# Eight conditioning units a layer ahead of the up phase, and 17 more value units by seven products

## What is computed

```python
# first block, layers i = 0, 1
x = x + mixed @ w_out[i]                       # mixer's output projection
h = rms_norm(x, norm2_w[i])
g, u = jnp.split(h @ w_up[i], [D_FF], axis=-1) # 1024 -> 2 * 2816
g = depthwise_conv_centered(g, ffn_conv_w[i], ffn_conv_b[i])
x = x + (jax.nn.silu(g) * u) @ w_down[i]       # 2816 -> 1024

# second block, layers i = 0..3; the conditioning c is the same for all tokens
shift1, scale1, gate1, shift2, scale2, gate2 = adaln(c, ada_w[i], ada_b[i])  # silu(c) @ w + b, 1024 -> 6 * 1024
h = x * (1.0 + scale1) + shift1
y = mixer_i(h)
x = layer_norm(DN_ALPHA * x + (1.0 + gate1) * y, ...)
h = x * (1.0 + scale2) + shift2
y = conv_ffn(h, ...)                           # gates and values both convolved
x = layer_norm(DN_ALPHA * x + (1.0 + gate2) * y, ...)
```

## Time and profile before

| | us |
|---|---|
| median of 3 runs | 2404.84 |
| lowest and highest | 2402.72, 2406.2 |
| profiled execution, its own time | 2405.74 |
| profiled execution, span in the trace | 2403.9 |
| TensorE busy in the span | 2379.8 |
| VectorE busy | 1636.7 |
| ScalarE busy | 729.3 |
| GpSimd busy | 151.8 |

### The profile page before, as it was taken

The page is one execution under the profiler, slowest core; times in us unless marked ns, Lnnn a source line. Parts: engine busy times, 40 slices in busy tenths (PEclk is TensorE's granted clock), DMA queues, the critical chain, the costliest instruction groups (busy, mean ns, idle before and its releaser), DMA issues.

```text
span 2403.9 us, 42597 instructions
## 1 busy us (share of the span) xinstructions
PE 2379.8 (99%) x17844; PEld 2186.9 (91%) x17844; DVE 1636.7 (68%) x3084; ACT 729.3 (30%) x1473; POOL 151.8 (6%) x268
## 2 busy tenths in 40 slices
PE   9999999999999999999999999999999999999998
PEld 7878999987899998999998899998899999889998
DVE  6653887566289947698744499954477984638983
ACT  3441220144321121533132243223423431544321
POOL 2000010000022000010000021021000000000000
PEclk9999999999999999999999999999999999999999
DMA  7935887574398756498654398754334555335542
GB/s 218 243 88 175 302 293 251 147 188 119 106 310 286 271 180 187 159 314 297 201 174 135 107 324 286 254 186 121 116 114 157 174 168 167 107 110 171 163 163 97
DMA packets 403273, 458.43 MB, mean 191 GB/s; under 512 B 50751, under 2 KB 374776, under 8 KB 403084
## 3 DMA queue, kind: packets, MB, share of 16 engines
q1 hardware_dynamic: 370098, 340.53, 45.4%
q0 software_dynamic: 29936, 112.73, 13.0%
q10 hardware_dynamic: 3050, 2.46, 0.4%
HBM read 451.48 MB, written 1.29 MB: 188 GB/s over the span
## 4 chain that ended last, share of the span: by engine, by line
PE 95%; DVE 2%; issue 1%; DMA 1%; ACT 0%; ACTq 0%; DVEq 0%; SPq 0%
PE job_bank L1034 34%; PE job_bank L1110 33%; PE job_bank L1089 11%; PE mix_bank L1089 4%; PE job_bank L1616 4%; PE mix_bank L1535 1%; PE job_bank L1118 1%; PE mix_bank L1563 1%; PE job_bank L1591 1%; PE mix_bank L1577 1%; PE mix_bank L1065 1%; PE mix_bank L1907 0%; PE job_bank L1340 0%; PE mix_bank L2011 0%; DMA sb_ring<-in_ffn_w_down 0%
## 5 line engine op out<-in xcount | busy, mean ns | idle before, releaser
L1034 PE MATMUL job_bank<-sb_h,sb_ring 128*128 128x256 f32 (+1 forms) x2880 | 645.8, 381 | 0.3 <-DVE sb_h L3375 0.3
L1034 PEld LDWEIGHTS job_bank<-sb_h,sb_ring 128*128 128x128 f32 (+1 forms) x2880 | 535.8, 189 | 83.3 <-issue 11.4
L3066 DVE SCALAR_TENSOR_TENSOR sb_arena<-sb_arena,sb_c_act 128x1024 f32<-128x1024 f32 x168 | 215.3, 1282 | 4.2
L3180 DVE SCALAR_TENSOR_TENSOR sb_arena<-sb_arena,sb_par 128x256 f32<-128x256 f32 x440 | 204.4, 505 | 8.8 <-ACT sb_arena L2189 4.9
L1110 PE MATMUL job_bank<-sb_t,sb_ring 128*128 128x128 f32 x1536 | 203.6, 275 | 1.2 <-DVE sb_ring L3116 1.2
L1110 PE MATMUL job_bank<-sb_h,sb_ring 128*128 128x128 f32 x1440 | 190.5, 275 | 0.0
L1110 PEld LDWEIGHTS job_bank<-sb_t,sb_ring 128*128 128x128 f32 x1536 | 187.3, 192 | 1.4 <-DVE sb_ring L3116 1.4
L1089 PE MATMUL job_bank<-sb_h,sb_ring 128*128 128x128 f32 x1600 | 184.1, 275 | 1.4 <-ACT sb_h L2502 1.4
L1110 PEld LDWEIGHTS job_bank<-sb_h,sb_ring 128*128 128x128 f32 x1440 | 179.2, 192 | 4.3 <-issue 1.6
L1089 PEld LDWEIGHTS job_bank<-sb_h,sb_ring 128*128 128x128 f32 x1600 | 181.2, 192 | 1.8 <-issue 1.6
L1110 PE MATMUL job_bank<-sb_t,sb_arena 128*128 128x128 f32 x1320 | 174.9, 275 | 0.8 <-DVE sb_arena L3121 0.8
(11 more groups left out here) (530 smaller groups left out, 3346.9 us busy)
## 6 DMA issues: line engine op xcount, KB each, us to landing
sb_arena<-in_ada_w POOLq DMA_DIRECT2D x96, 1024.0 KB, 7.1
sb_ring<-in_ffn_w_up SPq DMA_DIRECT2D x88, 1024.0 KB, 5.2
sb_ring<-in_w_up SPq DMA_DIRECT2D x44, 1024.0 KB, 7.1
sb_ring<-in_ffn_w_down SPq DMA_DIRECT2D x32, 1024.0 KB, 5.4
sb_ring<-in_w_in SPq DMA_DIRECT2D x24, 1024.0 KB, 6.6
sb_ring<-in_w_down SPq DMA_DIRECT2D x16, 1024.0 KB, 5.6
sb_ring<-in_hg_w_in SPq DMA_DIRECT2D x16, 1024.0 KB, 5.5
sb_ring<-in_ml_w_up SPq DMA_DIRECT2D x16, 1024.0 KB, 5.6
```

What stands on the lines that cost most here:

```text
L1034: mm = pe.matmul(o, st, mv, start=(k0 + k == 0 and t == 0), stop=(k0 + k == kn - 1), skip_group_check=True)
L3066: ins = vec.scalar_tensor_tensor(out=o, in0=w, scalar=col, in1=o, op0=ALU.mult, op1=ALU.add)
L3180: ins = vec.scalar_tensor_tensor(out=o, in0=fraw[:, i % 2, v, j:j + T], scalar=pcol(column, (l * FFN_TAPS + j) * width + c), in1=o, op0=AL ...
```

## The change

**Eight units early.** Of each layer's 24 conditioning units 8 (7 in the third layer, `ADA_EARLY`) are done before the up phase: for the first and second layer beside the mixer's output projection (5, 2 and 1 units ahead of the three additions to `x`); for the third layer 2 in the down phase of the second layer, 2 at the start of the conformer's mixer, 2 and 1 ahead of the additions of its output projection; for the fourth layer 2 in the down phase of the third, 2 and 2 in the HGRN2 mixer, 2 in its output projection. 12 (13 in the third) remain beside the up phase and 4 (`ADA_LATE`) beside the down phase. The early units of the first two layers have three buffers of their own, in a region that the scan has done with.

**The sums on TensorE** are placed by a rule now: the sums whose units are early come right after the first pair, the others four places behind the place at which VectorE is due to have counted the fourth, but no later than after the last unit (`min(p + 4, FT - 1)`). The sum of units 17 to 20 moves from the down phase to that last place.

**GpSimd** issues the loads of the early units when the first unit of the output projection is used, and `tap_loads` and `gate_loads` only after them. The products that follow stand directly behind these loads now, each ahead of the load of unit 8, 9 and so on.

**17 more fast value units.** 4 in each layer of the first block (values 1 to 9 are all fast), 5 in the second block's layer 0 (1, 3, 5, 7, 9) and 4 in its layer 1 (2, 4, 6, 8). In the second block VectorE joins such a value's tiles, where ScalarE copied them out of the bank before.

```diff
-ADA_BESIDE_UP = 20
+ADA_EARLY = (8, 8, 7, 8)
+ADA_LATE = 4
 FAST_FROM = 2
-FAST_VALUES = (1, 3, 5, 7, 9)
+FAST_VALUES = {1: ((1, 2, 3, 4, 5, 6, 7, 8, 9),) * L1, 2: ((1, 3, 5, 7, 9), (2, 4, 6, 8))}
...
+        def ada_place(layer, c):
+            if layer < L1 and c < ADA_EARLY[layer]:
+                return ADA_RING + c % ADA_RING
+            if c < ADA_EARLY[layer] or c >= ADA_UNITS - ADA_LATE:
+                return 1 + (c + 1) % 2
+            return c % ADA_RING
...
+        def ada_beside(layer, p):
+            beside = ADA_UNITS - ADA_EARLY[layer] - ADA_LATE
+            return p * beside // FT
+        def ada_ready(layer, count):
+            if count <= ADA_EARLY[layer]:
+                return -1
+            return next((p for p in range(FT) if ADA_EARLY[layer] + ada_beside(layer, p + 1) >= count), None)
...
                 if layer < L1:
                     ssd_rows(layer)
-                pool.wait_ge(s.tail_x, 2 * layer + 1)
-                if layer == L2 - 1:
-                    gate_loads()
-                if layer == L1 - 1:
-                    tap_loads()
+                    pool.wait_ge(s.unit_used, plan[("out1", layer)][0][1][0][0] + 1)
                 beside = tap_weights() if layer == L1 - 1 else gate_weights() if layer == L2 - 1 else iter(())
                 for c in range(ADA_UNITS):
+                    if layer == L2 - 1 and c == 6:
+                        pool.wait_ge(s.ho_read, 4)
+                    if c == ADA_EARLY[layer]:
+                        pool.wait_ge(s.tail_x, 2 * layer + 1)
+                        if layer == L2 - 1:
+                            gate_loads()
+                        if layer == L1 - 1:
+                            tap_loads()
                     if c >= 8:
                         next(beside, None)
...
+                layer = l if stack == 1 else l + 2
+                ready = [ada_ready(layer, 4 * (r + 1)) for r in range(ADA_UNITS // 4)]
                 def condition(n):
-                    if n in (8, 12, 17, 21):
-                        ada_quad()
+                    if n == 1:
+                        pe.wait_ge(s.tail_x, 2 * layer + 1)
+                    for p in ready:
+                        if p is not None and n == (1 if p < 0 else min(p + 4, FT - 1)):
+                            ada_quad()
...
                 first_products(d2, 2, *over_f(2))
-                ada_quad()
+                if ready.count(None) > 1:
+                    ada_quad()
...
                 for i, job in enumerate(plan[("out1", l)][:-1]):
+                    ada_units((5, 2, 1)[i])
                     add_to_x(job, i)
...
-            branch_out("pw2", 2, 0)
+            branch_out("pw2", 2, 0, (2, 1))
```

More of the change, by code:

```diff
@@ L466, in build @@
         zs = ssd(KD, T)
+        scanned_at = ssd.at
         yssm = ssd(KD, T)
@@ L505, in build @@
         ffn(8 * UC)
+        ffn(ARENA - ffn.at - (ADA_RING * 2 + 2) * ADA_COLS_AT_ONCE - UC)
         ada_w = ffn(ADA_RING, 2, ADA_COLS_AT_ONCE)
@@ L508, in build @@
         ada_rows = ffn(UC)
-        ada_buffer = [c % 3 if c < ADA_BESIDE_UP else 1 + (c + 1) % 2 for c in range(ADA_UNITS)] * L2
+        first_at = scanned_at - ADA_RING * 2 * ADA_COLS_AT_ONCE
+        ada_first = arena[:, first_at:scanned_at].rearrange("p (b k c) -> p b k c", b=ADA_RING, k=2)
+        def ada_place(layer, c):
[4 more added lines that the diff above has]
+            return c % ADA_RING
+        ada_buffer = [ada_place(layer, c) for layer in range(L2) for c in range(ADA_UNITS)]
+        ada_tile = [ada_w[:, b, :, :] if b < ADA_RING else ada_first[:, b - ADA_RING, :, :] for b in ada_buffer]
         ada_before = [max((m for m in range(n) if ada_buffer[m] == b), default=None) for n, b in enumerate(ada_buffer)]
-        ada_landed = [16 * ada_buffer[:n + 1].count(b) for n, b in enumerate(ada_buffer)]
+        ada_signal = [b % ADA_RING for b in ada_buffer]
+        ada_landed = [16 * ada_signal[:n + 1].count(b) for n, b in enumerate(ada_signal)]
         half_k = 4
@@ L655, in fast_up @@
             gates, values, _ = glu_jobs(stack, l)
-            if stack == 2 and l < FAST_FROM:
-                return gates[1:]
-            return [job for i in range(1, FT // 2)
-                    for job in (gates[i], values[i]) if job is gates[i] or stack == 2 or i in FAST_VALUES]
+            return [job for i in range(1, FT // 2) for job in (gates[i], values[i])
+                    if job is gates[i] or stack == 2 and l >= FAST_FROM or i in FAST_VALUES[stack][l]]
         def fast_down(stack, l):
@@ L1287, in fast_ups @@
                 heads(ups[:2], norm, before, ns)
+                after(1)
                 over_h = (h[:, :, :], hform, tform_no(stack, l))
@@ L3050, in ada_unit @@
                 n = ada_n[0]
-                vec.wait_ge(ada_in[ada_buffer[n]], ada_landed[n])
+                vec.wait_ge(ada_in[ada_signal[n]], ada_landed[n])
                 if n % 4 == 0 and n >= 8:
@@ L3056, in ada_unit @@
                 for k in range(2):
-                    w = ada_w[:, ada_buffer[n], k, :]
+                    w = ada_tile[n][:, k, :]
                     col = c_act[:, n % 4 * 2 + k:n % 4 * 2 + k + 1]
@@ L3078, in ada_copy @@
             def ada_copy():
-                vec.wait_ge(s.ada_summed, ada_n[0] // 4)
+                vec.wait_ge(s.ada_summed, ada_n[0] // ADA_UNITS * (ADA_UNITS // 4))
                 vec.tensor_copy(ada_rows[:, :], M[3][:, 0:UC]).then_inc(s.ada_copied, 1)
@@ L3223, in ahead @@
                         more_forms(1)
+                layer = l if stack == 1 else l + 2
                 def beside(p):
-                    ada_units((p + 1) * ADA_BESIDE_UP // len(ups) - p * ADA_BESIDE_UP // len(ups))
+                    ada_units(ada_beside(layer, p + 1) - ada_beside(layer, p))
                 ahead(2)
@@ L3251, in glu @@
                     else:
+                        if u[0] in fast_no:
+                            join_tiles(u, fraw[:, i % 2, 2:4, off:off + T])
                         ahead(2 * i + 4)
@@ L3276, in glu @@
                 more_forms(2)
-                ada_units(ADA_UNITS - ADA_BESIDE_UP - 2)
+                ada_units(ADA_LATE - 2)
                 vec.wait_ge(s.unit_used, done_units(downs[1]))
@@ L3283, in glu @@
                     gather(downs[1], 1)
+                if layer >= 1 and layer < L2 - 1:
+                    ada_units(2)
                 vec.wait_ge(s.unit_used, done_units(downs[2]))
@@ L3302, in glu, with branch_out @@
                     rescale_x(2 * l + 1)
-            def branch_out(name, ns, n):
+            def branch_out(name, ns, n, early=(0, 0)):
                 norm_columns(n)
                 for i, job in enumerate(plan[name][:-ns]):
+                    ada_units(early[i])
                     gated_to_x(job, i, n // 2, 0)
@@ L3714, in _ @@
             for i, job in enumerate(plan["hg_f"]):
+                ada_units((0, 0, 2, 2)[i])
                 read_out(vec, job)
@@ L3785, in _ @@
             due(s.h_ready, KD)
-            branch_out("hg_out", 2, 2)
+            branch_out("hg_out", 2, 2, (0, 2))
             glu(2, 1)
```

2 lines of the change are left out of this document (1 added, 1 removed).

## The result

The changed kernel takes 2423.62 us (median of 6 runs, 2423.12 to 2424.77); the kernel before, 2403.66 in 6 runs beside it. The ratio is 1.0083, with a 95% interval of 1.0071 to 1.0096: **20 us slower**. The forecast was 2415, range 2408.5 to 2424. The sign and the range held, and the middle was 8.6 us too low.

A forecast was written before the change was run, and what follows sets the result against it. TensorE, busy 2379.8 of 2403.9 us, was taken as the bound. The terms -11.0 + 18.4 + 0 + 0 + 0.7 + 2 = +10.1 us gave 2415 us, 0.42% slower, range 2408.5 to 2424.

The forecast's parts named there:

- The saving: TensorE in the up phases: each value unit converted to seven products saves 0.65 us, 17 of them 11.0 us.
- The added wait: Behind each up phase's last value unit, TensorE's sum waits for VectorE's unit 20: four times 4.6, 18.4 us lost.
- the whole down projection: TensorE's queue after each up phase: it stands behind the waiting sum, though it could start at once as before.
- The clock: TensorE's clock may fall in the four new waits: 2 us taken, bounds 0 and 9.2.
- the second rival: TensorE's clock falls at every wait, staying low about as long or longer: 9.2 us, total 2422; chance 0.17.
- the forecast's case: Whole kernel: the time falls between 2409.6 and 2419 us, around the forecast 2415; chance 0.58.
- The price at the upper bound: After the four waits, clock low as long again as each (4.6 us at half pace): 2.3 us each, 9.2 in all.
- GpSimd's products: Moved to the up phase's start, four meet VectorE's first weight sums in the second layer: 0 taken, bounds -2.8 and +4.
- the old 2.8 us: TensorE's idle time in the second layer's up phase, put down to GpSimd's mid-phase tap products; it can go.
- The early units: Eight conditioning units fit VectorE's idle spots before the up phases; only one spot is short: 0.7 us, bounds 0 and 2.
- The short spot in the conformer's output projection: A 2.70 us gap for a 2.5 us unit whose buffer comes free late: VectorE delayed 0 to 1.5, 0.7 taken.
- VectorE's load: Up phases: falls about 3 us net in three layers, rises nearly 4 in the third; 0 taken, bounds 0 and 4.

The follow-up runs named there:

- experiment 5: Changed kernel without the 17 further fast values, early units kept, sum of units 17 to 20 back in the down phase: 2406.82 us, ratio 1.0013 to the kernel before.
- experiment 1: Changed kernel with the sum of units 17 to 20 back in the down phase, early units and fast values kept: 2395.62 us, ratio 0.9965 to the kernel before.
- experiment 4: Kernel before with only the sum of units 17 to 20 moved to behind the last value unit: 2428.45 us, ratio 1.0101.
- experiment 3: Changed kernel with the sum of units 17 to 20 six matmuls into the down phase's first job (wait 1.9 us): 2404.56 us, ratio 1.0004 to the kernel before.
- Experiment 7: Kernel of experiment 1 with GpSimd's products later in the second and fourth layers' up phases: 2389.42 us, ratio 0.9938 to the kernel before.
- Experiment 6: Kernel before with the 17 further fast values and the second block's join alone, no early units: 2443.07 us, ratio 1.0162.
- experiment 2: Changed kernel with 20 unread identity matmuls ahead of the sum behind the last value unit, filling TensorE's wait: 2417.51 us.
- experiment 9: Changed kernel with the sum of units 17 to 20 three matmuls into the down phase's first job (wait 3.2 us): 2414.22 us, ratio 1.005 to the kernel before.

## Why the prediction was right, and where it was off

**The saving** (11.0 us) was right: 0.65 us a value in the rows of the first layer (experiment 5), and experiments 5 and 1 differ by 11.2.

**The added wait** (18.4 us) was right: 17.9 us, four times 4.5, at the four places. That it was VectorE's order and not its load is shown by experiment 4, where the load is that of the kernel before. What the prediction called the whole down projection queued behind the sum is shown by experiments 3 and 1: put behind 2.6 us of that work, the wait is 1.9 us, and in the down phase it is none.

**The clock** is the term that was mis-sized: 2 us taken, bounds 0 and 9.2, and 9.7 measured. This is nearly the whole miss (2415 + 7.7 = 2422.7, measured 2423.6). The bounds nearly held it; the choice between them did not, and the second rival, with 0.17, came out at 2422: it, and not the forecast's case, describes what happened. The step that failed is the choice of 2 us out of 0 to 9.2, and its ground, the sentence "No row shows matmuls at the lower level". That the range still held is owed to that rival's place in it. The trace of before has such rows, late in the program, in the stick-breaking attention, and I had not looked there:

```profile
2088.00:2092.00 4.00, 2.29 (x21) 2.10 (x19) 3.83 (x6) 3.04 (x4) 0.00 (x0) 1.00 0.00 1
2092.00:2096.00 4.00, 3.68 (x14) 3.32 (x15) 1.23 (x2) 1.70 (x2) 0.00 (x0) 0.57 0.00 0
...
2092.32 1.22 PE L2011 MATMUL mix_bank<-sb_arena,sb_from_s 128*128 128x256 f32 x2 [2.03 <-DVE sb_arena L3951]
...
2098.94 0.60 PE L2011 MATMUL mix_bank<-sb_arena,sb_from_s 128*128 128x256 f32 x2
```

Behind a wait of 2.03 us the next 4 us ran at 0.57 and a matmul took 1.22 us that takes 0.60 at the full clock. (The profile of the changed kernel has a stretch as long behind the same wait, so it is no part of the 9.7.) With this row the low end would not have been the natural choice for waits more than twice as long. The row that I used instead, the full clock at 2395 to 2399 with a nearly idle TensorE, has TensorE busy for 1.27 of 4 us, which is no case of dense work behind a wait. The price at the upper bound was nearly right: as long again as the wait at half pace was 9.2 us, against 9.7 measured, though the single places differ (behind 4.5 us the clock stayed low for 3 to 6 us).

The Trainium skill, "TensorE: Matmul & The Clock Gate", section "Why this matters for your kernels", warns of idle gaps between bursts of matmuls, because the clock then falls. By that rule it falls in all four waits, and the trace agrees (0.53 to 0.61 behind each). The runs also show falls behind waits of about 2 us, and there they decide.

**GpSimd's products** were taken at 0, bounds -2.8 and +4. In the second layer the old 2.8 us of waits (three, at 735 to 745 us) went and 4.0 came (2.3 + 1.7), net 1.2. In the fourth, 1.6 us came (1.1 + 0.5) that I had called "within the same bounds" and put at 0. Both were inside, but the two halves of the term should not have been netted into nothing: the prediction itself described the collision (four products meet the first weight sums), and the row of 2.65 us for an operation of 0.28 said how hard it is. Experiment 7 shows that this was worth 6 us, by removing it.

**The early units** fitted, as forecast. The short spot in the conformer's output projection cost 0.4 us (a wait of 1.05 us in the place of the 0.63 in the earlier trace rows), where 0.7 was taken. Between the second layer's down phase and there, two waits of 0.8 and 0.9 us went and one of 0.9 came, 0.8 us less that I had not foreseen, and their cause was not looked into.

**VectorE's load** was taken at 0, and that held: in the changed kernel the only waits for it in the up phases are those above, and the third layer, where the load was to rise by 4 us, has none but that of the sum. Experiment 6 gives the other side: without the early units the same conversions cost 39 us.

The sum with the measured terms: -11.0 + 17.9 + 9.7 + 1.2 + 1.6 + 0.4 - 0.8 = +19.0 us; the two profiled spans differ by 19.0. So close a match is luck in the last few tenths: single waits of 0.6 us come and go elsewhere.

## What to carry to other kernels

When a step of the bounding engine is moved, look at which instance of another engine's work it waits for, and count that engine's program back from there; a rule of the form "n places later" must not be cut off at the end of the loop. Price a new wait of the matmul engine of several microseconds at its length and add a second term for the lower clock behind it (here 2.4 us on average behind 4.5), and look through the whole trace for a dip before you call that unlikely. Early, cheap work in a queue also moves what stands behind it: GpSimd's products that slipped to the start of a phase cost 5.6 us of waits, 2.8 net of those that went, where the early units cost 0.4 in their own places.

## What the runs showed of the hardware

- TensorE's clock behind the four waits for the sum, in otherwise dense work: it fell at none of four places behind 1.9 us, at three of four behind 3.2, and at all four behind 3.9 (experiment 4) and 4.5; with 4.6 us of matmuls in the place of the wait of 4.5, at none. At the start of the second layer's up phase it fell behind the wait of 3.4 us in all three profiles that have one (experiments 2, 5 and 9), and not behind 2.3 us (changed kernel, experiments 1 and 3).
- Near 2 us it is not certain either way. Late in the program (2092.32 us in the kernel before) all 11 profiles have the same wait of 2.0 us; the clock fell behind it in 7 of them and held in experiments 2, 3, 6 and 9. In experiment 6 it fell behind one wait of 1.92 us and held behind another. It fell once, at 1504 us there, behind two waits of 0.97 and 0.83 us that stand 2 us apart, so a wait need not be long by itself.
- The wait of 3.85 us at the very start of the program, ahead of the first matmul, had no fall behind it in the kernel before.
- Low stretches of the granted clock cost about half their length in matmuls: by the clock 9.7 us over the four places, by TensorE's busy time 9.8 (2378.0 against 2368.2). A sum takes 1.08 us instead of 0.64, a matmul 1.22 instead of 0.60.
- A GpSimd product of 2 us stretches VectorE's sums of two tensors in SBUF by about its own length each: 0.68 to 2.45 us beside one product, 0.69 to 5.38 beside two.
